# Gate, up and down products of a two-FFN layer as seven block products for eight

## The chip, the cores and the metric

The kernel runs on one core of a Trainium2 chip. The metric is device time in microseconds (us) of one launch. A core has a matrix engine (TensorE, PE), three engines for elementwise work (VectorE or DVE, ScalarE or ACT, GpSimd or POOL) and a queue engine (SyncE, SP) that issues the DMAs between DRAM and the on-chip memory SBUF. Matmuls write to eight PSUM banks of 128 x 512 fp32 words. Each engine runs its own instruction stream in order; semaphores order the engines against each other.

## What is computed

One layer over x of 1024 tokens x 1024 features, all fp32:

```
x = x + 1/2 * swiglu(rmsnorm(x, ffn1_norm), ffn1 weights)
x = x + attention(rmsnorm(x, mix_norm))       # 16 query heads, 4 key heads, window of 2 chunks of 64, sinks
x = x + 1/2 * swiglu(rmsnorm(x, ffn2_norm), ffn2 weights)
out = rmsnorm(x, final_norm)
swiglu(h) = (silu(h @ w_gate) * (h @ w_up)) @ w_down      # w_gate, w_up 1024 x 2816, w_down 2816 x 1024
```

## The kernel before

Every product is made with three passes of the engine's reduced fp32 type (fp32r): an operand is split into a high half (ACT copies it into fp32r) and a low half (DVE subtracts the high half from it), and high x high, high x low and low x high are added up in PSUM (`three_passes`, L391 is the matmul). The tokens are 8 tiles of 128, and two halves of 512.

An FFN is a loop over 11 groups of 256 hidden columns (`swiglu` on each engine). SP loads the 1024 x 256 blocks of the gate and up weights into `stage_g` and `stage_u` and 256 rows of the down weights into `stage_d`; ACT and DVE split them into `w` (`hi_of` L647, `lo_of` L951). PE makes four units per group (two column blocks f, two token halves), each of 48 matmuls: gate into one bank, up into another (`gate_up_unit`). For each unit `hidden` follows: ACT takes silu of the gate bank (L691), DVE multiplies it with the up bank (L1011), ACT and DVE split the result into `a_T` (L694, L1015). Then PE makes the group's share of the down product, 16 units of 6 matmuls (`down_unit`, 8 token tiles, 2 column halves), through a ring of four banks, and DVE adds each to x, which stays in SBUF (`add_to_x`, L1022). The first unit of the next group is put behind the down product.

Norms (index m, 8 tiles each for FFN1, attention, FFN2 and the end) are spread over four engines: POOL multiplies the tile of x with the norm's weights (`weigh`, L341), ACT sums the squares (L663) and takes the root (L668), DVE corrects it (`rstd`, L972 to L978), ACT or DVE scales (L675, L984), PE transposes by the identity (`turn`, L418), ACT and DVE split into `hT` (L683, L1003). The tiles of the first norm are interleaved with the first group's products; those of the attention's norm follow as the last group's tiles come out of the down product; those of FFN2's norm are turned while the attention's output product runs (`o_unit`), the last three inside `first_gate_up`. Attention itself (q, k, v products, scores, exp, probabilities times v, output product) is written out by hand as an interleaving of 16 steps, and its order is not touched by the change.

## Time and profile before

| | us |
|---|---|
| median of 3 runs | 1812.92 (1812.62 to 1813.11) |
| profiled execution, span from first to last instruction | 1812.2 |
| PE busy in it | 1760.0 (97%) |
| DVE busy | 809.5 (45%) |
| ACT busy | 493.7 (27%) |
| POOL busy | 133.0 (7%) |
| bytes moved by the DMA queues | 101.85 MB |

The profile is of one execution. Its own time is the span; what lies around it is the 0.7 us by which the median stands above. The engines work side by side, so the busy times don't add up to the span; what matters is which engine the others wait for. Start times in the rows are counted from the span's start. A few per cent of the matmul records can be missing, so a count in a timeline row may be a little short.

### The profile page before, as it was taken

How to read it: one execution, taken by the hardware profiler on the slowest of the kernel's cores; microseconds unless marked ns; L12 is line 12 of the kernel's file. 1: busy time of each engine (PE TensorE's matmuls, PEld its weight loads, DVE VectorE, ACT ScalarE, POOL GpSimd, SP SyncE). 2: the span in 40 equal slices, each digit the busy share in tenths (PEclk: the TensorE clock that was granted, in tenths of full speed). 3: DMA queues.
4: the chain of work that ended last, by engine and by line, in shares of the span. 5: the costliest groups of instructions: out<-in, count | busy, mean ns of one | idle time of the engine just before them, and what ended most of it. 6: DMA issues, size and time to landing. Idle time of an engine off the chain costs nothing.

```text
span 1812.2 us, 20835 instructions
## 1 busy us (share of the span) xinstructions
PE 1760.0 (97%) x8200; PEld 1464.0 (81%) x8200; DVE 809.5 (45%) x1226; ACT 493.7 (27%) x918; POOL 133.0 (7%) x82
## 2 busy tenths in 40 slices
PE   5999999999999999889999999999999999999996
PEld 4888888888888888778888878888888888888885
DVE  7433323424423332743689984343234244233326
ACT  4211111122111111532666653111111221111114
POOL 4000000000000000440221320000000000000003
PEclk9999999999999999999999999999999999999999
DMA  5212102102102201133212232121021021022002
GB/s 177 81 59 69 46 23 69 46 23 69 53 17 69 81 23 24 36 80 84 59 47 59 59 93 74 66 69 46 23 69 46 23 69 47 22 69 81 0 1 93
DMA packets 103751, 101.85 MB, mean 56 GB/s; under 512 B 37792, under 2 KB 93216, under 8 KB 103712
## 3 DMA queue, kind: packets, MB, share of 16 engines
q1 hardware_dynamic: 103712, 101.34, 18.3%
q8 instruction: 24, 0.39, 0.1%
q14 instruction: 15, 0.12, 0.0%
HBM read 97.13 MB, written 4.19 MB: 56 GB/s over the span
## 4 chain that ended last, share of the span: by engine, by line
PE 86%; DVE 11%; ACT 1%; issue 1%; DMA 0%; DVEq 0%; ACTq 0%
PE bank L391 84%; DVE x_res L1022 2%; DVE w L951 2%; DVE stat L978 2%; DVE hT L1003 1%; DVE stat L972 1%; PE bank L418 1%; PE bank L563 1%; DVE hT L1171 1%; DVE soft L1133 1%; DVE probs_T_lo L1158 1%; DVE hn L984 0%; PE bank L576 0%; ACT hT L683 0%; ACT junk L663 0%
## 5 line engine op out<-in xcount | busy, mean ns | idle before, releaser
L391 PE MATMUL bank<-hT,w 128*128 128x512 f32 (+1 forms) x4728 | 1078.8, 389 | 3.0 <-DVE hT L1003 1.6
L391 PEld LDWEIGHTS bank<-hT,w 128*128 128x128 f32 x4728 | 883.7, 188 | 186.2 <-issue 3.1
L391 PE MATMUL bank<-w,a_T 128*128 128x512 f32 x2112 | 484.7, 390 | 3.2 <-DVE x_res L1022 3.2
L391 PEld LDWEIGHTS bank<-w,a_T 128*128 128x128 f32 x2112 | 395.8, 188 | 86.9 <-DVE x_res L1022 4.9
L1011 DVE TENSOR_TENSOR a_full<-silu_g,bank 128x512 f32<-128x512 f32 x88 | 60.5, 688 | 682.8 <-ACT silu_g L691 682.6
L1022 DVE SCALAR_TENSOR_TENSOR x_res<-bank,x_res 128x512 f32<-128x512 f32 x416 | 278.0, 688 | 140.8 <-PE bank L391 140.5
L691 ACT ACTIVATE silu_g<-bank 128x512 f32<-128x512 f32 x88 | 52.7, 599 | 696.2 <-PE bank L391 696.2
L341 POOL TENSOR_TENSOR hn<-x_res,norm_w 128x1024 f32<-128x1024 f32 x31 | 77.8, 2521 | 1474.2 <-DVE x_res L1022 1454.3
L647 ACT ACTIVATE w<-stage_d 128x1024 fp32r<-128x1024 f32 x60 | 61.1, 1062 | 357.5 <-PE bank L391 357.5
L391 PE MATMUL bank<-w,hT 128*128 128x512 f32 (+1 forms) x576 | 120.3, 364 | 1.5 <-DVE x_res L1022 1.0
L391 PEld LDWEIGHTS bank<-w,hT 128*128 128x128 f32 x576 | 95.6, 194 | 17.4 <-DVE w L951 2.1
L1015 DVE TENSOR_TENSOR a_T<-a_full,a_T 128x512 fp32r<-128x512 f32 x88 | 61.0, 693 | 61.4 <-ACT a_T L694 61.4
L951 DVE TENSOR_TENSOR w<-stage_d,w 128x1024 fp32r<-128x1024 f32 x60 | 79.2, 1353 | 8.9 <-ACT w L647 8.7
L694 ACT ACTIVATE a_T<-a_full 128x512 fp32r<-128x512 f32 x88 | 55.6, 632 | 66.4 <-DVE a_full L1011 66.4
L418 PE MATMUL bank<-ident,hn 128*128 128x128 f32 x192 | 29.3, 302 | 31.6 <-DVE hn L984 19.1
L951 DVE TENSOR_TENSOR w<-stage_g,w 128x1024 fp32r<-128x1024 f32 x44 | 54.4, 1235 | 5.5 <-ACT w L647 5.2
L418 PEld LDWEIGHTS bank<-ident,hn 128*128 128x128 f32 x192 | 24.3, 155 | 37.5 <-issue 17.7
L951 DVE TENSOR_TENSOR w<-stage_u,w 128x1024 fp32r<-128x1024 f32 x44 | 53.6, 1219 | 0.0
L800 ACT ACTIVATE probs<-bank,soft 128x128 f32<-128x128 f32 (+1 forms) x128 | 45.0, 372 | 25.4 <-DVE soft L1137 25.4
L647 ACT ACTIVATE w<-stage_g 128x1024 fp32r<-128x1024 f32 x44 | 46.0, 1046 | 0.0
L647 ACT ACTIVATE w<-stage_u 128x1024 fp32r<-128x1024 f32 x44 | 45.9, 1044 | 0.0
L364 POOL TENSOR_TENSOR probs<-probs,soft_inv 128x512 f32<-128x512 f32 x32 | 33.9, 1068 | 109.9 <-DVE soft_inv L1146 109.6
(62 smaller groups left out, 675.7 us busy)
## 6 DMA issues: line engine op xcount, KB each, us to landing
stage_d<-in_ffn_w_down SPq DMA_DIRECT2D x22, 1024.0 KB, 4.9
stage_g<-in_ffn_w_gate SPq DMA_DIRECT2D x21, 1024.0 KB, 5.4
stage_u<-in_ffn_w_up SPq DMA_DIRECT2D x21, 1024.0 KB, 7.9
stage_d<-in_attn_w_o SPq DMA_DIRECT2D x32, 256.0 KB, 3.9
stage_qkv<-in_attn_w_qkv SPq DMA_DIRECT2D x32, 256.0 KB, 3.7
x_res<-in_x SPq DMA_DIRECT2D x8, 512.0 KB, 6.7
stage_qkv<-in_attn_w_qkv SPq DMA_DIRECT2D x8, 512.0 KB, 3.7
out_dram<-hn SPq DMA_DIRECT2D x7, 512.0 KB, 2.6
```

The costliest lines, as they stand in the source:

```text
L341: pool.tensor_tensor(hn[:, m % 4, :], x_res[:, t, :], norm_w[:, :], ALU.mult).then_inc(weighted, 1)
L391: mm = pe.matmul(psum, lhs, rhs, start=(first and n == 0 and v == 0), stop=(last and n == len(parts) - 1 and v == 2))
L418: mm = pe.transpose(banks[turn_bank(m) + k // 4][:, (k % 4) * P:(k % 4 + 1) * P], hn[:, m % 4, k * P:(k + 1) * P], ident[:, :])
L647: act.activation(slot_view, stage, ACT.Copy).then_inc(hi_done, 1)
L691: act.activation(silu_g[:, half, :], banks[2 * half][:, :], ACT.Silu).then_inc(silu_done, 1)
L694: act.activation(a_T[:, 0, f, half * HALF:(half + 1) * HALF], a_full[:, half, :], ACT.Copy).then_inc(a_hi_done, 1)
L800: act.activation(probs[:, b % 4, n, lo:], banks[s][:, n * P + lo:(n + 1) * P], ACT.Exp, bias=soft[:, NEG_MAX, b % 4, n:n + 1], accum_out=s ...
L951: dve.tensor_tensor(lo, stage, hi.bitcast(F32), ALU.subtract).then_inc(split_done, 1)
L978: dve.tensor_tensor(stat[:, RSTD, c], stat[:, R0, c], stat[:, CORR, c], ALU.mult).then_inc(rstd_done, tiles)
L1011: dve.tensor_tensor(a_full[:, half, :], silu_g[:, half, :], banks[2 * half + 1][:, :], ALU.mult).then_inc(gate_up_free, 1)
L1015: dve.tensor_tensor(a_T[:, 1, f, cols], a_full[:, half, :], a_T[:, 0, f, cols].bitcast(F32), ALU.subtract).then_inc(a_ready, 1)
L1022: dve.scalar_tensor_tensor(out=cols, in0=banks[4 + bank_][:, :], scalar=factor, in1=cols, op0=ALU.mult, op1=ALU.add).then_inc(ring_free, 1)
```

## The change

The three large products of each FFN are made by Strassen's scheme in Winograd's form. The left operand is cut into 2 x 2 blocks (A11, A12, A22 and the sums S1 to S4; A21 enters only in sums), the right one likewise, and seven products of forms (product k takes form k, in the order A11, A12, S2, S3, S1, A22, S4) give all four result blocks, summed in two PSUM banks with copies between.

- *Gate and up.* The normed activations, 1024 tokens x 1024, are cut at 512 tokens and 512 features. Their seven forms (`forms`, 128 x 7 x 2 x 4 x 512) are built once per FFN: POOL makes S3, S2, S1, S4 in natural order (`natural_sums`), PE transposes each 128 x 512 piece (`turn_unit`, 28 per FFN), ACT and DVE split it. The tiles are normed in place in x_res (the first four) and in hn, so x is loaded again later, in FFN2 from a copy that is written to DRAM (`x_mid`, `spill_x`). The weight forms of each group are built by DVE from the stages (`slot_sums`) and split (`slot_hi_of`, `slot_lo_of`). A group is 14 steps (7 products k, 2 matrices m) of 12 matmuls. ACT copies a running sum from its bank (`copy_part`), DVE adds the other bank to it (`sum_block`), then silu and product give the four hidden blocks (`silu_block`, `hidden`).
- *Seven forms of the hidden activations.* DVE makes the sums (`hidden_sums`, `hidden_last_sum`), and SP stores all seven forms of each group to DRAM (`hidden_forms`), 256 KB each.
- *Down.* It is no longer part of the groups but a phase behind all 11 of them: 7 products of 11 steps, each step 12 matmuls over four banks (`down`, `down_tile`). SP loads the hidden block of each step back through a ring of six; the whole down matrix is loaded in four quarters (`load_down_w`), and POOL makes their sums (`down_sums`, 44 of 128 x 512 per FFN). The last six steps run tile by tile. x gets 28 additions per FFN (`add_down`) for 176.
- The tiles 0 to 3 and 4 to 7 finish at different products, and the norm behind each FFN follows that order.

The core of the diff:

```diff
+PRODUCTS = 7
+HI_BEFORE = [0, 2, 6, 4, 8, 10, 12]
+LO_BEFORE = [0, 2, 8, 4, 6, 10, 12]
+STEPS = PRODUCTS * GROUPS
+SPLITS = 6
+LAST_STEPS = STEPS - SPLITS
+DOWN_TO = [(0, 0), (0, 0), (1, 0), (1, 1), (1, 1), (1, 0), (0, 1)]
...
@@ sync
-            def load_groups(gate, up, down, s0):
-
-                with sp.Fori(0, GROUPS - 1) as i:
-                    sp.wait_ge(split_done, i * 6 + (s0 + 4))
-                    load_gate_up(gate, up, i * GROUP + GROUP)
-                    sp.wait_ge(split_done, i * 6 + (s0 + 6))
-                    load_down(down, i * GROUP + GROUP)
+            def group(q, i, g0):
+                sp.wait_ge(slot_ready, nth(i, 14, 14 * (GROUPS * q + g0 + 1)))
+                load_stage(q, i * GROUP + (g0 + 1) * GROUP)
+                for part in range(3):
+                    stores(q, i, g0, part)
...
+                for n in range(SPLITS, STEPS):
+                    down_consumed(sp, q, n - SPLITS)
+                    if n == SPLITS or n % GROUPS == 0:
+                        sp.wait_ge(buf_stored[BUF_OF[n // GROUPS]], 16 * GROUPS * (q + 1))
+                    load_a(q, n)
+                    if n in (6, 10, 14):
+                        load_down_w(q, B12, (n - 6) // 4)
+                    if n in (8, 12, 16):
+                        load_down_w(q, B22, (n - 8) // 4)
+                    if n in (7, 9, 11, 13, 24, 26, 28, 30):
+                        half, j = divmod([7, 9, 11, 13, 24, 26, 28, 30].index(n), 4)
+                        t = j + 4 * (half if q else 1 - half)
+                        if q:
+                            sp.wait_ge(spilled[t], 16)
+                        load_x(source, t)
...
@@ gpsimd
+            def natural_sums(q, j):
+                n = 16 * q + 4 * j
+                h1, h2 = h_of(q, N_FFN[q] + j), h_of(q, N_FFN[q] + 4 + j)
+                pool.wait_ge(hn_done, N_FFN[q] + 4 + j + 1)
+                if j:
+                    pool.wait_ge(form_turned, UNITS * q + 8 + 5 * j)
+                pool.tensor_tensor(nat[:, NAT_OF[S3], :], h1[:, 0:HALF], h2[:, 0:HALF], ALU.subtract
+                                   ).then_inc(nat_done, 1)
...
+            def first_forms(q):
+                for j in range(6):
+                    weigh_form(q, j)
+                natural_sums(q, 0)
+                weigh_form(q, 6)
+                natural_sums(q, 1)
+                weigh_form(q, 7)
+                natural_sums(q, 2)
+                natural_sums(q, 3)
...
+            def down_sums(q):
+                done = 4 * GROUPS * q
+                ready = 2 * STEPS * q
+                for g in range(GROUPS):
+                    pool.wait_ge(down_w_loaded[B12][g // 4], 16 * (q + 1))
+                    pool.wait_ge(down_w_loaded[B22][g // 4], 16 * (q + 1))
+                    pool.tensor_tensor(down_w[B12][:, g, :], down_w[B22][:, g, :], down_w[B12][:, g, :], ALU.subtract
+                                       ).then_inc(down_w_summed, 1)
+                    pool.wait_ge(down_w_summed, done + 2 * g + 1)
+                    pool.wait_ge(down_ready, ready + 2 * (g + 1))
+                    pool.tensor_tensor(down_w[B11][:, g, :], down_w[B12][:, g, :], down_w[B11][:, g, :], ALU.add
+                                       ).then_inc(down_w_summed, 1)
...
@@ tensor
+                if k == 0 and first and q:
+                    pe.wait_ge(exp_done, 32)
+                elif k == 0 and not first:
+                    pe.wait_ge(hidden_done if m else silu_done, nth(i, 4, 4 * n))
+                elif k == 1 and not first:
+                    pe.wait_ge(block_summed, nth(i, 6, 6 * n - 1 + m))
+                elif k in (2, 4, 6):
+                    pe.wait_ge(part_copied, nth(i, 6, 6 * n + k - 1 + m))
+                elif k in (3, 5):
+                    pe.wait_ge(block_summed, nth(i, 6, 6 * n + k - 2 + m))
+                three_passes(banks[y_bank if k in (1, 3, 5) else x_bank][:, :],
+                             [((slot[q][k][m][:, 0, kt, :], slot[q][k][m][:, 1, kt, :]),
+                               (forms[:, k, 0, kt, :], forms[:, k, 1, kt, :])) for kt in range(4)],
+                             k in (0, 1, 3), k in (1, 5, 6)).then_inc(gate_up_done, 1)
...
+            def down(q, between):
+                for n in range(LAST_STEPS):
...
+                    pe.wait_ge(down_ready, 2 * STEPS * q + 2 * (n + 1))
+                    for j in range(4):
+                        down_tile(q, n, j)
+                for j in range(4):
+                    if between is not None:
+                        between(j)
+                    for n in range(LAST_STEPS, STEPS):
+                        if j == 0:
+                            pe.wait_ge(down_ready, 2 * STEPS * q + 2 * (n + 1))
+                        down_tile(q, n, j)
...
@@ vector
+            def group(q, i, g0, first=False, last=False):
+                if not first:
+                    sum_block(q, i, g0, 0, 0)
+                    sum_block(q, i, g0, 0, 1)
+                hidden(q, i, g0, 0)
+                if not last:
+                    slot_lo_of(q, i, g0 + 1, 0)
+                    slot_lo_of(q, i, g0 + 1, 1)
+                    slot_sums(q, i, g0 + 1, 3)
+                    slot_sums(q, i, g0 + 1, 2)
+                sum_block(q, i, g0, 1, 0)
+                sum_block(q, i, g0, 1, 1)
+                hidden(q, i, g0, 1)
...
+            for n in range(TT):
+                if n < 5:
+                    down_lo_of(1, 72 + n)
+                if n >= 4:
+                    add_down(1, 6, n - 4)
+                variance(N_FINAL + n)
+                rstd(N_FINAL + n)
```

## Rows read from the trace of the kernel before

**Rows 1.** Page, parts 1 and 2: busy us, share, instructions; PE in 40 slices.

```profile
PE 1760.0 (97%) x8200; PEld 1464.0 (81%) x8200; DVE 809.5 (45%) x1226; ACT 493.7 (27%) x918; POOL 133.0 (7%) x82
...
PE   5999999999999999889999999999999999999996
```

**Rows 2.** Page, part 4: the chain of waits by engine and by line.

```profile
PE 86%; DVE 11%; ACT 1%; issue 1%; DMA 0%; DVEq 0%; ACTq 0%
PE bank L391 84%; DVE x_res L1022 2%; DVE w L951 2%; DVE stat L978 2%; DVE hT L1003 1%; DVE stat L972 1%; PE bank L418 1%; PE bank L563 1%; DVE hT L1171 1%; DVE soft L1133 1%; DVE probs_T_lo L1158 1%; DVE hn L984 0%; PE bank L576 0%; ACT hT L683 0%; ACT junk L663 0%
```

**Rows 3.** Timeline of PE, 100 to 235 us: start, length, instructions, idle before.

```profile
144.00 21.92 PE L391 MATMUL bank<-w,a_T 128*128 128x512 f32 x96
165.76 43.68 PE L391 MATMUL bank<-hT,w 128*128 128x512 f32 x192
209.28 21.92 PE L391 MATMUL bank<-w,a_T 128*128 128x512 f32 x96
```

**Rows 4.** Groups by line and shape: busy us, mean ns, idle before and its releaser.

```profile
L1015 DVE TENSOR_TENSOR a_T<-a_full,a_T 128x512 fp32r<-128x512 f32 x88 | 61.0, 693 | 61.4 <-ACT a_T L694 61.4
L694 ACT ACTIVATE a_T<-a_full 128x512 fp32r<-128x512 f32 x88 | 55.6, 632 | 66.4 <-DVE a_full L1011 66.4
...
L951 DVE TENSOR_TENSOR w<-stage_g,w 128x1024 fp32r<-128x1024 f32 x44 | 54.4, 1235 | 5.5 <-ACT w L647 5.2
...
L364 POOL TENSOR_TENSOR probs<-probs,soft_inv 128x512 f32<-128x512 f32 x32 | 33.9, 1068 | 109.9 <-DVE soft_inv L1146 109.6
```

**Rows 5.** Timeline of ACT and of DVE in one group.

```profile
176.84 0.60 ACT L691 ACTIVATE silu_g<-bank 128x512 f32<-128x512 f32 x1 [7.57 <-PE bank L391]
...
177.47 0.69 DVE L1011 TENSOR_TENSOR a_full<-silu_g,bank 128x512 f32<-128x512 f32 x1 [8.06 <-ACT silu_g L691]
```

**Rows 6.** DMA issues (KB, us to landing); window 0 to 20 (last: DMA share, GB/s).

```profile
stage_g<-in_ffn_w_gate SPq DMA_DIRECT2D x21, 1024.0 KB, 5.4
stage_u<-in_ffn_w_up SPq DMA_DIRECT2D x21, 1024.0 KB, 7.9
...
0.00:20.00 20.00, 2.59 (x11) 2.22 (x12) 13.50 (x17) 6.73 (x14) 12.70 (x11) 1.00 0.97 305
```

**Rows 7.** Timeline of the start, POOL and PE.

```profile
6.74 12.00 POOL L341 TENSOR_TENSOR hn<-x_res,norm_w 128x1024 f32<-128x1024 f32 x5 [5.27 <-DMA norm_w<-in_ffn_norm]
...
45.92 24.35 PE L391 MATMUL bank<-hT,w 128*128 128x512 f32 x106 [0.91 <-DVE hT L1003]
```

**Rows 8.** Timeline of PE between FFN1 and the q and k products.

```profile
777.70 1.97 PE L418 MATMUL bank<-ident,hn 128*128 128x128 f32 x8 [5.40 <-DVE hT L1003]
...
779.32 5.09 PE L391 MATMUL bank<-w,hT 128*128 128x256 f32 x24
...
784.25 1.04 PE L418 MATMUL bank<-ident,hn 128*128 128x128 f32 x8
...
785.05 3.12 PE L391 MATMUL bank<-w,hT 128*128 128x256 f32 x24
...
788.00 12.20 PE L391 MATMUL bank<-hT,w 128*128 128x512 f32 x53
```

**Rows 9.** Timeline where the attention's output product ends and FFN2 starts.

```profile
1065.00 1.06 ACT L663 ACTIVATE junk<-x_res 128x1024 f32<-128x1024 f32 x1 [1.55 <-DVE x_res L1022]
...
1072.37 1.64 PE L391 MATMUL bank<-w,hT 128*128 128x512 f32 x6
...
1086.11 14.09 PE L391 MATMUL bank<-hT,w 128*128 128x512 f32 x61
```

**Rows 10.** Timeline of the end: the last addition to x.

```profile
1804.17 0.67 DVE L1022 SCALAR_TENSOR_TENSOR x_res<-bank,x_res 128x512 f32<-128x512 f32 x1
```

**Rows 11.** Timeline of DVE and POOL where both work.

```profile
735.54 4.55 DVE L951 TENSOR_TENSOR w<-stage_qkv,w 128x1024 fp32r<-128x1024 f32 x2
...
735.71 3.30 POOL L341 TENSOR_TENSOR hn<-x_res,norm_w 128x1024 f32<-128x1024 f32 x1 [702.36 <-DVE x_res L1022]
...
1778.56 4.77 POOL L341 TENSOR_TENSOR hn<-x_res,norm_w 128x1024 f32<-128x1024 f32 x2 [700.50 <-DVE x_res L1022]
...
1780.01 0.69 DVE L1022 SCALAR_TENSOR_TENSOR x_res<-bank,x_res 128x512 f32<-128x512 f32 x1
```

More of the change, by code:

```diff
@@ new lines, in trunk @@
+    probs_T_lo = at("probs_T_lo", 204, [P, 2, 4 * P], F32R)
+    norm_w = at("norm_w", 208, [P, D])
+    q_T = {key: at(f"q_T{key[0]}{key[1]}", 96 + 8 * slot, [P, HALF // CHUNK, 4, CHUNK])
+           for key, slot in Q_SLOT.items()}
+    forms = at("forms", 32, [P, PRODUCTS, 2, 4, HALF], F32R)
+    stage = [at("stage_g", 144, [P, KD, GROUP]), at("stage_u", 152, [P, KD, GROUP])]
+    early = [[168, 172], [176, 180], [160, 164]]
+    low, high = [[0, 4], [8, 12]], [[16, 20], [24, 28]]
+    slot_kb = [early + low + high, early + high + low]
@@ L206, in trunk, with nth, h_of, down_consumed @@
         wo_view = w_o.rearrange("(i s e p) n -> i s e p n", i=2, s=2, e=4)
+        def nth(i, per, start):
+            return i * per + start
+        def h_of(q, m):
+            j = m - N_FFN[q]
+            return x_res[:, tile_of(m), :] if j < 4 else hn[:, j - 4, :]
+        def down_consumed(engine, q, n):
+            p, g = divmod(n, GROUPS)
+            if g == GROUPS - 1:
+                engine.wait_ge(down_full, 28 * q + 4 * p + 4)
+            else:
+                engine.wait_ge(down_step, (LAST_STEPS - 6) * q + (GROUPS - 1) * p + g + 1)
         block = ctx.enter_context(nc.Block())
@@ new lines, in feed_forward @@
+            def feed_forward(q):
+                first_pairs(q)
+                group(q, 0, 0, first=True)
+                with act.Fori(0, GROUPS - 2) as i:
+                    group(q, i, 1)
+                group(q, 0, GROUPS - 1, last=True)
+            act.wait_ge(started, 1)
+            act.activation(stat[:, R0, 0:1], stat[:, RSTD, 0:1], ACT.Sqrt)
+            for j in range(4):
+                act.wait_ge(x_loaded[tile_of(j)], 16)
+                square_to(j, junk[:, :])
+                if j >= 1:
+                    root(j - 1)
+                if j >= 2:
+                    scale_in(j - 2, h_of(0, j - 2))
@@ L744, in _ @@
+            root(3)
+            form_hi_of(0, 0)
+            form_hi_of(0, 1)
+            scale_in(2, h_of(0, 2))
+            form_hi_of(0, 2)
+            form_hi_of(0, 3)
+            scale_in(3, h_of(0, 3))
+            for v in range(4, 8):
+                form_hi_of(0, v)
+            slot_hi_of(0, 0, 0, 0, True)
+            slot_hi_of(0, 0, 0, 1, True)
+            feed_forward(0)
             loads = [0, 0]
@@ new lines, in _ @@
+            scale_mix(1)
+            down_hi_of(0, 74)
+            root(N_MIX + 2)
+            square_mix(3)
+            scale_mix(2)
+            down_hi_of(0, 75)
+            root(N_MIX + 3)
+            scale_mix(3)
+            down_hi_of(0, 76)
+            hi_qkv(0)
+            hi_qkv(1)
+            norm_back(0)
+            norm_back(1)
+            for t in range(4, TT):
+                square_mix(t)
+                root(N_MIX + t)
+                if t < 6:
+                    norm_back(t - 2)
+                scale_mix(t)
+                if t >= 6:
+                    norm_back(t - 2)
@@ L774, in shift_v @@
+            hi_qkv(2)
+            norm_back(6)
+            norm_back(7)
             def shift_v(half):
@@ new lines, in feed_forward @@
+            def feed_forward(q):
+                group(q, 0, 0, first=True)
+                with dve.Fori(0, GROUPS - 2) as i:
+                    group(q, i, 1)
+                group(q, 0, GROUPS - 1, last=True)
+                for n in range(SPLITS, 72):
+                    if n % GROUPS == SPLITS and n > SPLITS:
+                        for j in range(4):
+                            add_down(q, n // GROUPS - 1, j)
+                    down_lo_of(q, n)
+                for j in range(4):
+                    add_down(q, 5, j)
```

1225 lines of the change are left out of this document (727 added, 498 removed).

## The prediction

> **What bounds the kernel now.** I read the page's busy times first [rows 1]: TensorE (PE) is busy for 97% of the span, and the 40 slices show full stretches broken only at the start, between 720 and 780 us, and at the end. VectorE (DVE) is at 45%, ScalarE (ACT) at 27%. The chain of waits agrees [rows 2]: 86% of it is PE, 84% the three-pass matmuls of L391. So the kernel is bound by the number of 128x512 matmuls, and everything else counts only where PE waits. The PE timeline gives the price [rows 3]: from 165.76 to 209.28 us run 192 gate and up matmuls, from 144.00 to 165.76 run 96 down matmuls, both at 226.67 ns each with no gap. A group of 256 hidden columns is 288 of them, 65.28 us; one FFN is 11 groups, 718.1 us.
>
> **What the seven products remove.** A group has 7 products x 2 matrices x 4 contraction tiles x 3 passes = 168 matmuls of the same shape for 192. The down product, now a phase after all groups, has 7 x 11 steps x 4 tiles x 3 passes = 924 for 1056. One FFN falls from 3168 to 2772, or 396 x 0.22667 = 89.8 us; two give **-179.5**. An FFN's floor is 628.3 us.
>
> **The group loop, cost 0.** A group is 14 steps of 12 matmuls, 2.72 us each, 38.08 in all. DVE gets 36 instructions of 128x512 (14 low halves, 8 weight sums, 6 block sums, 4 products, 4 hidden sums); at 0.69 [rows 4] that is 24.8 us. ACT gets 24, 15.1 us at 0.63 [rows 4], with one table load. Neither fills 38.08, and POOL is idle, so the order of the waits decides. The tightest is product 5 after product 4: the running sum must be copied from its bank (ACT) and added to the other bank (DVE) before PE may write that bank, while PE has one step, 2.72 us, in between. The trace has such a handoff: a unit that PE left at 176.64 is read by ACT from 176.84, and DVE starts at 177.47, 0.03 after ACT ended [rows 5]. So 0.20 + 0.63 + 0.69 = 1.5 us, slack 1.2. I followed both queues in program order over one group, with the sums of the next group's weights between; each arrives 1.2 us or more before PE needs it. The weights of the next group are asked for 5.6 us into a group, land at 11 and 13.5 by the landing times [rows 6], and are wanted at 17. Bounds: 0, and 1 us a group (22 us) where that slack is used up; I take 0, as the handoffs of the loop of before never reach PE [rows 3].
>
> **The first group of each FFN, +7.** There the previous group's tail does not exist: the last slot is ready only about 17 us into the group, the 2 MB land 8 us later, and ACT's copies and DVE's sums stand behind them in their queues. Product 5 then starts at 30.8 us of group time for 27.2, 3.6 us late, twice. Bounds 0 and 12.
>
> **The start of FFN1, +20.** Before, PE went on with the second unit at 45.92, having done 48 matmuls (10.9 us): effective start 35.0 [rows 7]. After, product 2 needs all four S2 forms, and these come from POOL: 8 norm products of 128x1024, 2.40 each (five in 12.00) [rows 7], and 16 half-width sums. The trace has no such sum: half of 2.40 is 1.20, the 128x512 product with soft_inv took 1.07 [rows 4]; I take 1.20. ACT carries squares, scales, eight form copies and four slot copies before the second four tiles; with the DVE steps between held up by POOL that is an estimate of 28 us. Two more norm products end at 34.3, the first scaled tile of the second half stands at 35.6, then POOL has 16 x 1.20 + 2 x 2.40 = 24.0 to do: 59.6, and product 2 starts 2 us later (slot split). Four steps of PE are done by then: effective start 50.7, +15.7. Against it: DVE has twelve instructions with both inputs in SBUF in this stretch, 8.3 us, that exclude POOL (next part); I take 3. And PE has idled: after 5.40 us of idle the next 24 matmuls of 128x256 took 5.09 where 24 later took 3.12 [rows 8], 1.2 for 2.4 GHz; I take 1.3. Sum +20. Lower bound 13 (1.07 each, no interference), upper 27.
>
> **The start of FFN2, +17.** Before, the remaining units start at 1086.11, effective start 1075.2, and the attention's output product ended at 1074.0: the next norm was hidden but for 1.2 us [rows 9]. After, tile 4 is squared from 1065.00 as now [rows 9], two norm products and a held-up DVE step put the first scaled tile at 1073.2, and the same 24.0 us of POOL end at 1097.2. With 2 for the slot, 3 for interference and 1 for the clock, less 10.9 for four steps under it: 1092.3, +17. Bounds 10 and 24. This is cover that the old order had and the new one gives up.
>
> **Into attention, -15.** Before, FFN1's work would have ended at 35.0 + 718.1 = 753.1, and the q and k products start at 788.00 [rows 8], 34.9 us later, for 4 v units (785.05 to 788.00: 2.95) and 8 transposed tiles (784.25 to 785.05: 0.80), 18.2 us. The rest is PE waiting for norms of tiles that end 2.72 us apart. After, tiles 0 to 3 are complete one product (30 us) earlier, and the last four end 4.1 us or more apart, about the 4 us that a norm takes, with v units between. I take 15 of the 16.7; bounds 10 and 17. **The end, -10.** Before, from 1075.2 + 718.1 = 1793.3 to 1812.2 is 18.9. After, four tiles are normed early and the last add starts 0.3 after PE; from the last add's start to the end were 8.0 us [rows 10]. With 0.6 of queue 8.9. Bounds 7 and 10.6. The attention between is the same: 0.
>
> **The down phase, +10 an FFN, +20.** A step is 2.72 us; DVE has 2 instructions for it (1.4 us), ACT 2. Three things are late there.
> (a) Transfers, 4: between steps 6 and 16 SP issues 11 hidden blocks (2.9 MB), 6 chunks of down weights (5.8 MB) and 4 tiles of x (2.1 MB), 10.8 MB in 27 us, behind some 9 us of backlog. The fullest stretch of before moved 305 GB/s at a DMA share of 0.97 [rows 6]; 10.8 MB take 35 us. The six-deep ring covers all but about 4. Bounds 0 and 5.
> (b) POOL against DVE, 3. At 735.54 DVE's two low halves took 4.55 (2 x 1.24 on the mean [rows 4]) while POOL's product took 3.30 for 2.40: one waited for the other, then the other way round [rows 11]. An add from PSUM took its 0.69 under a running POOL product [rows 11]. So an instruction with both inputs in SBUF and a POOL sum exclude each other. All of this phase's low halves are such, and POOL has 44 sums: while POOL has work, two DVE instructions cost up to 2 x (1.20 + 0.69) = 3.8 us for a step of 2.72. The ring hides some, chunk arrivals space POOL. Bounds 0 and 9.
> (c) Product 6, 3: the last five steps' low halves stand between the norms of four finished tiles, whose POOL products hold DVE 2.4 each; all six last steps must be ready for the first tile. Followed in order, the last is ready up to 5.5 late. Bounds 0 and 5.5.
> Together 0 to 20 an FFN, I take the middle, 10. The Trainium skill (DMA: Bandwidth & Descriptors, Specifications) puts the limit of a core's memory at about 358 GB/s. By that (a) would be nothing and the sum 8 lower; the 305 of the row is the measured one, and stands.
>
> **Sum.** 1812.2 - 179.5 + 7 + 20 + 17 - 15 - 10 + 20 = 1671.7 against the profiled execution, whose span of 1812.2 is 0.7 under the median of 1812.92. Forecast **1672 us**, 7.8% less. All lower bounds together give 1629, all upper ones 1741.
>
> **Rivals.** *Everything covered* (0.12): POOL's chain at its lower bounds, a down phase without a stall: 1812.9 - 179.5 + 13 + 10 - 17 - 10 + 4 = 1633. For it: the slack of PE's neighbours. Against: the chains of the starts are counted instructions on one engine.
> *The down phase paced by DVE behind POOL* (0.15): 44 POOL sums each paired with one DVE instruction are 83 us, in which DVE serves 22 steps, 60 us of PE: 23 lost, with (a) and (c) 33 an FFN, so 1672 + 2 x 23 = 1718. For it: the row at 735.54. Against: POOL waits for chunks and for split steps, so its sums don't stand back to back. The Trainium skill (SBUF — State Buffer, Who interferes with whom) calls this an exclusive lock held for a whole instruction; the trace agrees, 4.55 us for 2.4.
> *The group loop held by queue order* (0.12): 2 us a group where one late copy delays product 5, 22 x 2 = 44, 1716. For it: 36 + 24 instructions in two strict orders. Against: the slack of 1.2 us.
> *Slower than before* (0.02): DVE bound in the group loop. Break-even is a group of 38.08 + 141/22 = 44.5 us, or 1.24 us for each of the 36 instructions in place of 0.69; at 1.32 it would be 47.5 and the kernel 1879. For it: they read stages in pieces of 128 columns, never in the trace at this width. Against: a low half over such pieces at twice the width took 1.24 [rows 4], and half the width should not take the same.
> *The matmuls do not fall as counted, or each takes longer* (0.01): 1812.
>
> **Chances.** My forecast, with 1650 to 1700 as its own range, has 0.58. The range for 8 in 10 is 1640 to 1720: it cuts most of the covered case and ends just beyond the two dear ones. Within 0.2% (3.6 us) is what a measurement can't tell from no change. Faster 0.97, same 0.01, slower 0.02.
>
> **What would show it.** Right: 2772 matmuls per FFN at 0.227; loop groups of 38.1 us; PE waiting at both starts for forms whose maker is POOL; the q and k products under 20 us after FFN1's last; in the down phase, PE waits on DVE low halves in steps 9 to 30 and 71. Wrong: a loop group above 39 us, starts later than 27 us beyond the old ones, or down phases over 230 us (floor 209.4).

## The result, and the profile after

| | before | after |
|---|---|---|
| median (lowest to highest) of four runs each, us | 1813.01 (1812.62 to 1814.69) | 1727.25 (1725.97 to 1728.17) |
| span of the profiled execution, us | 1812.2 | 1724.0 |

The ratio of the times is 0.9524, 95% interval 0.9511 to 0.9538: 4.8% faster, where 7.8% was forecast. The forecast's span of 1671.7 us was missed by 52.3, and 1727 lies beyond the range of 1640 to 1720.

The page of the kernel after: busy times, PE in 40 slices, the chain of waits by engine, and four groups (busy us, mean ns, idle before).

```profile
PE 1625.4 (94%) x7480; PEld 1336.9 (78%) x7480; DVE 1114.5 (65%) x1752; ACT 725.2 (42%) x1463; POOL 311.3 (18%) x202
...
PE   4799999999998999799999996999999999989996
...
PE 74%; DVE 18%; ACT 3%; DMA 3%; issue 2%; POOL 0%; DVEq 0%; SPq 0%; ACTq 0%
...
L573 PE MATMUL bank<-forms,slot 128*128 128x512 f32 x3696 | 849.6, 392 | 9.6 <-DVE slot L1347 5.8
...
L573 PE MATMUL bank<-b_ring,a_ring 128*128 128x512 f32 x1848 | 437.6, 396 | 24.6 <-DVE b_ring L1391 24.5
...
L1388 DVE TENSOR_TENSOR a_ring<-a_raw,a_ring 128x512 fp32r<-128x512 f32 x154 | 142.6, 926 | 125.0 <-ACT a_ring L938 125.0
...
L1391 DVE TENSOR_TENSOR b_ring<-down_w,b_ring 128x512 fp32r<-128x512 f32 x154 | 144.5, 938 | 0.0
```

3696 and 1848 matmuls are 2772 an FFN, as counted. PE's share fell from 97% to 94%, with shallow dips at both starts, in both down phases, behind FFN1 and at the end, and DVE's part of the chain rose from 11% to 18% [rows 1, 2]. The place to look stands in the last two groups: a low half of 128x512 takes 0.93 us on the mean, where the same shape took 0.69 before [rows 4]. The two groups hold 308 of them, and PE waited 24.5 us for them.

PE's timeline gives a ledger. "Effective start" is the time at which an FFN would have begun had its 11 groups run at 38.08 us each up to the first down matmul. Every line is in us of the profiled executions.

| stretch | predicted | measured | off |
|---|---|---|---|
| effective start of FFN1, first group included | 58.5 | 486.33 - 418.9 = 67.4 | +8.9 |
| down phase of FFN1, its four transposed tiles (3.2) included | 222.6 | 486.33 to 725.08: 238.8 | +16.1 |
| to the q and k products | 16.7 | 725.08 to 745.16: 20.1 | +3.4 |
| q and k to the end of the output product | 286.0 | 288.8 | +2.8 |
| from there to the effective start of FFN2 | 21.7 | 1033.97 to 1066.0: 32.0 | +10.3 |
| down phase of FFN2 | 219.4 | 1484.91 to 1715.7: 230.8 | +11.4 |
| the end | 8.9 | 8.3 | -0.6 |
| sum | | | +52.3 |

So 27.5 of the 52.3 are in the two down phases and 19.2 in the two starts. Inside FFN1's down phase the loss sits in two places. The first: PE between 525 and 561 us (start, length, count, idle before), then DVE and POOL in 5 us of it.

```profile
525.35 3.02 PE L573 MATMUL bank<-b_ring,a_ring 128*128 128x512 f32 x12 [0.37 <-DVE b_ring L1391]
...
540.30 3.02 PE L573 MATMUL bank<-b_ring,a_ring 128*128 128x512 f32 x12 [0.39 <-DVE b_ring L1391]
...
560.70 9.59 PE L573 MATMUL bank<-b_ring,a_ring 128*128 128x512 f32 x41 [0.34 <-DVE b_ring L1391]
```

```profile
536.38 1.61 POOL L519 TENSOR_TENSOR down_w<-down_w,down_w 128x512 f32<-128x512 f32 x1
536.77 1.77 DVE L1388 TENSOR_TENSOR a_ring<-a_raw,a_ring 128x512 fp32r<-128x512 f32 x1
...
537.96 1.75 POOL L515 TENSOR_TENSOR down_w<-down_w,down_w 128x512 f32<-128x512 f32 x1
...
538.47 1.78 DVE L1391 TENSOR_TENSOR b_ring<-down_w,b_ring 128x512 fp32r<-128x512 f32 x1
...
540.17 1.77 DVE L1388 TENSOR_TENSOR a_ring<-a_raw,a_ring 128x512 fp32r<-128x512 f32 x1
...
541.36 18.74 POOL L524 TENSOR_TENSOR down_w<-down_w,down_w 128x512 f32<-128x512 f32 x11
```

A step takes 3.40 us instead of 2.72. DVE's low halves start every 1.70 us, and between two of their starts lies exactly one start of a POOL sum: the two engines take turns, one instruction each. POOL's last back-to-back sum ends at 560.1 (541.36 and 18.74), and the row at 560.70 is the first with no further gap. The second place is product 6, the last six steps: PE there, then DVE ahead of the first wait and in a later step.

```profile
692.28 1.94 PE L701 MATMUL bank<-ident,hn 128*128 128x128 f32 x8 [3.45 <-ACT hn L872]
...
698.46 0.96 PE L573 MATMUL bank<-b_ring,a_ring 128*128 128x512 f32 x3 [0.40 <-DVE b_ring L1391]
702.88 1.65 PE L573 MATMUL bank<-b_ring,a_ring 128*128 128x512 f32 x3 [3.46 <-DVE b_ring L1391]
707.05 1.65 PE L573 MATMUL bank<-b_ring,a_ring 128*128 128x512 f32 x3 [2.52 <-DVE b_ring L1391]
```

```profile
683.49 2.88 DVE L1391 TENSOR_TENSOR b_ring<-down_w,b_ring 128x512 fp32r<-128x512 f32 x1
686.90 1.75 DVE L1281 SCALAR_TENSOR_TENSOR stat<-stat 128x1 f32<-128x1 f32 x1 [0.27 <-ACT stat L865]
...
688.88 2.08 DVE L1287 TENSOR_TENSOR stat<-stat 128x1 f32<-128x1 f32 x1
...
697.11 0.69 DVE L1388 TENSOR_TENSOR a_ring<-a_raw,a_ring 128x512 fp32r<-128x512 f32 x1 [2.00 <-ACT a_ring L938]
```

PE waits for the first normed tile, then for each step's low half. Up to 690.93 POOL's norm products (four in 10.33 us from 680.60) hold DVE up to 2.9 us an instruction, a product of one column among them. From then on the low halves have their 0.69 again, and it is the order of the queues that delays them: ACT makes a step's high halves only behind the square and the scaling of a tile, DVE waits 2.00 us for them (the row at 697.11), and the steps come 4.2 to 4.4 us apart. After the long waits three matmuls took 1.65 us, at a granted clock of 0.50 (1.2 GHz), where three took 0.96 after a short one, at 1.00 (2.4 GHz); the mean from 688.70 to 725.08 was 0.77.

### The profile page after: what moved, and what is told of

It reads as the page before. It is cut to its first block, busy times and chain, and to the rows that moved or that the text cites. A ratio compares the mean times of both kernels' runs of the same rounds, so it can differ in the third digit from the quotient of the medians.

```text
span 1724.0 us, 22342 instructions
## 1 busy us (share of the span) xinstructions
PE 1625.4 (94%) x7480; PEld 1336.9 (78%) x7480; DVE 1114.5 (65%) x1752; ACT 725.2 (42%) x1463; POOL 311.3 (18%) x202
## 4 chain that ended last, share of the span: by engine, by line
PE 74%; DVE 18%; ACT 3%; DMA 3%; issue 2%; POOL 0%; DVEq 0%; SPq 0%; ACTq 0%
PE bank L573 71%; DVE b_ring L1391 4%; DVE a_ring L1388 3%; DVE x_res L1627 1%; DVE slot L1347 1%; DMA a_raw<-hidden_forms 1%; DVE w L1268 1%; DVE forms L1305 1%; DMA stage_u<-in_ffn_w_up 1%; DVE stat L1281 1%; DVE stat L1287 1%; PE bank L773 1%; DVE x_res L1403 1%; DVE hT L1616 1%; DVE soft L1579 1%
## 5 line engine op out<-in xcount | busy, mean ns | idle before, releaser
L573 PE MATMUL bank<-forms,slot 128*128 128x512 f32 x3696 | 849.6, 392 | 9.6 <-DVE slot L1347 5.8
L573 PEld LDWEIGHTS bank<-forms,slot 128*128 128x128 f32 x3696 | 699.9, 190 | 157.5 <-DVE slot L1347 7.0
L573 PE MATMUL bank<-b_ring,a_ring 128*128 128x512 f32 x1848 | 437.6, 396 | 24.6 <-DVE b_ring L1391 24.5
L573 PEld LDWEIGHTS bank<-b_ring,a_ring 128*128 128x128 f32 x1848 | 349.2, 191 | 110.9 <-DVE b_ring L1391 39.1
L1388 DVE TENSOR_TENSOR a_ring<-a_raw,a_ring 128x512 fp32r<-128x512 f32 x154 | 142.6, 926 | 125.0 <-ACT a_ring L938 125.0
L1391 DVE TENSOR_TENSOR b_ring<-down_w,b_ring 128x512 fp32r<-128x512 f32 x154 | 144.5, 938 | 0.0
L1347 DVE TENSOR_TENSOR slot<-raw,slot 128x512 fp32r<-128x512 f32 x176 | 116.5, 713 | 1.6 <-ACT slot L902 1.6
L573 PE MATMUL bank<-hT,w 128*128 128x512 f32 x480 | 113.7, 393 | 0.0
L573 PEld LDWEIGHTS bank<-hT,w 128*128 128x128 f32 x480 | 88.8, 188 | 19.2 <-DVE w L1268 0.3
L902 ACT ACTIVATE slot<-raw 128x512 fp32r<-128x512 f32 x176 | 98.2, 622 | 0.1
```

Source lines behind the costliest of these rows:

```text
L573: mm = pe.matmul(psum, lhs, rhs, start=(first and n == 0 and v == 0), stop=(last and n == len(parts) - 1 and v == 2), skip_group_check=True)
L902: act.activation(slot[q][k][m][:, 0, :, :], src, ACT.Copy).then_inc(slot_hi, 1)
L1347: dve.tensor_tensor(slot[q][k][m][:, 1, :, :], src, slot[q][k][m][:, 0, :, :].bitcast(F32), ALU.subtract).then_inc(slot_ready, 1)
L1388: dve.tensor_tensor(a_ring[r][:, 1, :], a_raw[r][:, :], a_ring[r][:, 0, :].bitcast(F32), ALU.subtract).then_inc(down_ready, 1)
L1391: dve.tensor_tensor(b_ring[r][:, 1, :], src, b_ring[r][:, 0, :].bitcast(F32), ALU.subtract).then_inc(down_ready, 1)
```

## The experiments

Each kernel is the one after with the edit shown. Its lines may be moved by a few. A time without a range is of one execution; four executions of one of these kernels lie 1.4 to 3.4 us apart, so differences of 2 us are read from the rows and not from the times.

**e1: fills with zero in place of the down sums**, so this kernel leaves the 44 sums of an FFN out.

```diff
-                    pool.tensor_tensor(down_w[B12][:, g, :], down_w[B22][:, g, :], down_w[B12][:, g, :], ALU.subtract
-                                       ).then_inc(down_w_summed, 1)
+                    pool.memset(down_w[B12][:, g, :], 0.0).then_inc(down_w_summed, 1)
...
```

> The 44 sums of down weights per FFN on POOL are replaced by fills of the same tiles with zero (same waits, same counts, nothing read), so the down product is not the reference's. Theory A (exclusion): a POOL instruction that reads SBUF and a DVE instruction with both inputs in SBUF shut each other out. Then DVE's low halves of the ring fall from 1.78 to 0.69 us in steps 7 to 24, PE's steps 14 to 24 from 3.40 to 2.72, and each down phase is 9 us shorter: 1727 - 18 = 1709 (1706 to 1712). Rival B (transfers): the ring ran empty because of the loads between steps 6 and 16; the fills change nothing there: 1727. Rival C (results): PE waits for the sums' results; the fills are shorter but come at the same chunk landings: 1722 to 1727.

Measured: 1707.76 us, span 1705.7: theory A. **e2: the same sums on DVE**, each ahead of or behind the low halves of the step that frees its block, POOL without them; this kernel computes the whole layer.

```diff
                 for n in range(SPLITS, 72):
+                    p, g = divmod(n, GROUPS)
+                    if p == 1:
...
+                        w_sum(B12, g, B22, B12, ALU.subtract, 0)
+                    if p == 2:
+                        w_sum(B21, g, B21, B11, ALU.subtract, 2 * g + 2, GROUPS + g + 1)
...
                     down_lo_of(q, n)
+                    if p == 1:
+                        w_sum(B11, g, B12, B11, ALU.add, 2 * g + 1, g + 1)
+                    if p == 3:
+                        w_sum(B12, g, B22, B11, ALU.subtract, 2 * g + 2, n + 1)
```

> The same 44 sums moved from POOL to DVE, between its low halves, one or two per step (complete kernel). Theory A (exclusion): DVE has 2 low halves and at most 2 sums per step, 4 x 0.69 = 2.8 us in product 1 where the ring was 5 steps ahead, 2.1 after; nothing excludes it any more. Down phases 7 to 9 us shorter each: 1709 to 1713. Rival B (transfers set it): 1727 or more, since DVE now also waits for the chunks. If DVE's own queue becomes the limit in product 1 (11 x 0.1 us and the waits): 1714 to 1720.

Measured: 1708.75 us, span 1707.0, theory A again, and once more:

> The same kernel as e2_dve_sums (the 44 sums of an FFN's down weights on DVE in place of POOL), timed in three rounds: 1708 to 1710 us, ratio to the kernel before 0.942, interval wholly below that of the change itself (0.9511 to 0.9538).

Measured: 1708.41 us (1707.2 to 1708.6, four runs), ratio to before 0.9418 (0.9402 to 0.9433), against 0.9511 to 0.9538 for the change. First PE in e1, and DVE where POOL's memsets run; then PE and DVE in e2 (its second run), in the same stretch; then two windows of e2 (busy of PE, PEld, DVE, ACT, POOL; granted clock, DMA share, GB/s).

```profile
485.85 84.48 PE L569 MATMUL bank<-b_ring,a_ring 128*128 128x512 f32 x372
...
532.43 0.53 POOL L522 MEMSET down_w<- 128x512 f32 x1 [2.03 <-DVE b_ring L1387]
...
532.78 0.69 DVE L1384 TENSOR_TENSOR a_ring<-a_raw,a_ring 128x512 fp32r<-128x512 f32 x1 [0.47 <-ACT a_ring L934]
```

```profile
486.01 84.26 PE L571 MATMUL bank<-b_ring,a_ring 128*128 128x512 f32 x371
...
533.72 0.68 DVE L1389 TENSOR_TENSOR b_ring<-down_w,b_ring 128x512 fp32r<-128x512 f32 x1
534.32 1.28 DVE L1491 TENSOR_TENSOR down_w<-down_w,down_w 128x512 f32<-128x512 f32 x2
```

```profile
486.00:525.35 39.35, 39.35 (x175) 32.59 (x174) 25.43 (x43) 14.55 (x27) 0.00 (x0) 1.00 0.98 356
525.35:560.70 35.35, 35.35 (x158) 29.27 (x157) 33.80 (x57) 14.87 (x27) 0.00 (x0) 1.00 0.49 157
```

In both, PE runs without a gap from the first down matmul; the rows end with the window asked for, and in FFN1 the first wait comes only after 71 of the 77 steps, 193 us on. That holds though DVE is busy 96% of the second window in e2. The same 44 additions cost 9.2 us an FFN on an engine that seemed free and nothing in PE's rows on the one that seemed loaded: on DVE a sum takes 0.64 (two in 1.28), on POOL it took 1.7 and made one low half 1.77 long for 0.69. The transfers were the same in e1 and e2, so they were not the cause.

**e3: high and low halves of the last steps ahead of the norms**, on ACT and DVE, and PE's transposes behind each tile instead of ahead of it.

```diff
                 for j in range(4):
-                    if between is not None:
-                        between(j)
                     for n in range(LAST_STEPS, STEPS):
...
+                    if between is not None:
+                        between(j)
...
+            for n in range(72, STEPS):
+                down_lo_of(0, n)
             for t in range(4):
-                down_lo_of(0, 72 + t)
                 variance(N_MIX + t)
```

> In product 6 the high and low halves of steps 72 to 76 are put before the norms of the four finished tiles, on ACT and DVE; on PE the transposes of these norms come after each tile's steps instead of before (FFN1). Theory N (norm queue): the last six steps lose 16.9 us in FFN1 and 12.1 in FFN2 (6.9 of waits, the rest at the lower clock after them); both fall to 0 to 4: 1727 - 24 = 1703 (1699 to 1709). Rival (the norms only move the wait): PE then waits at the transposes in FFN1 for as long, and gains only in FFN2: 1715.

Measured: 1725.23 us, span 1723.2, above theory N's 1703 and its rival's 1715. The theory fell as a sum, though its step came true: PE ended product 6 at 715.1 instead of 725.2. It then stood idle. PE in e3 behind FFN1, and DVE's additions to x at the end of FFN2:

```profile
710.74 4.35 PE L573 MATMUL bank<-b_ring,a_ring 128*128 128x512 f32 x18
...
723.54 5.49 PE L573 MATMUL bank<-w,hT 128*128 128x256 f32 x24 [7.58 <-DVE x_res L1396]
...
745.81 14.57 PE L573 MATMUL bank<-hT,w 128*128 128x512 f32 x63
```

```profile
1704.48 0.69 DVE L1396 SCALAR_TENSOR_TENSOR x_res<-bank,x_res 128x512 f32<-128x512 f32 x1
1708.05 0.69 DVE L1396 SCALAR_TENSOR_TENSOR x_res<-bank,x_res 128x512 f32<-128x512 f32 x1
...
1715.19 0.69 DVE L1396 SCALAR_TENSOR_TENSOR x_res<-bank,x_res 128x512 f32<-128x512 f32 x1
```

The additions come at the pace of the norms ahead of them in DVE's queue, 3.57 us a tile, from 1704.48 on (1696.61 in the next kernel, where they stand earlier). PE ended 4.9 us sooner, at 1711.0, and from there to the end it took 12.2 us for 8.2. The q and k products start at 745.81, no sooner than the 745.16 of the kernel after, and attention took 2 us longer, in the wait for an addition to x ahead of the last of the output product (5.35 us for 4.03) and at the lower clock behind it (12 matmuls in 5.43 us for 4.58); why that wait was longer stays open. **e7: e3, and these additions one norm step earlier.**

```diff
+                if t in (1, 3):
+                    add_down(0, 6, t // 2)
...
             for n in range(TT):
-                if n >= 4:
-                    add_down(1, 6, n - 4)
                 variance(N_FINAL + n)
+                if n in (3, 4, 6):
+                    add_down(1, 6, {3: 1, 4: 2, 6: 3}[n])
                 rstd(N_FINAL + n)
+                if n == 1:
+                    add_down(1, 6, 0)
```

> The kernel e3_lo_first (high and low halves of the last five steps ahead of the norms) with one more edit: the adds that take product 6 out of its banks stand one norm step earlier on DVE, so they no longer wait behind the scaling factor of another tile. In e3 the PE's waits inside product 6 had gone, and after the last tile PE stood idle 7.58 us at 723.54 behind the last add at 722.79, and at the end the first add came only at 1704.48, six us after its tile, with the others 3.57 us apart. Theory D (the gain of e3, about 10 us in FFN1 and 5 in FFN2, was given back at the handover by the order of DVE's queue): the v units start at about 717.5 in place of 723.5 and the final chain ends about 8.3 us after PE's end (1710.8), 4 us sooner: span 1723.2 - 4 for the tail, and up to - 5 for attention: 1714 to 1719. Rival N (the handover is paced by the norm chain of the tiles itself, about 4.6 us a tile on ACT and DVE, whatever the adds do): only the tail's 4 us or less, and q and k products start where they did, span 1719 to 1723.

Measured: 1719.93 us, span 1717.9. That is in theory D's range, but not by its steps. DVE's first and last addition at the end, then PE behind FFN1:

```profile
1696.61 0.69 DVE L1396 SCALAR_TENSOR_TENSOR x_res<-bank,x_res 128x512 f32<-128x512 f32 x1
...
1709.89 0.69 DVE L1396 SCALAR_TENSOR_TENSOR x_res<-bank,x_res 128x512 f32<-128x512 f32 x1
```

```profile
712.08 1.10 PE L701 MATMUL bank<-ident,hn 128*128 128x128 f32 x8 [1.89 <-DVE hT L1515]
...
723.53 5.46 PE L573 MATMUL bank<-w,hT 128*128 128x256 f32 x24 [5.36 <-issue]
...
744.46 15.91 PE L573 MATMUL bank<-hT,w 128*128 128x512 f32 x69
```

PE now ends at 1707.5, 10.4 us before the end: the tail is 1.8 us shorter than in e3, where 4 were forecast, and still 2.2 longer than in the kernel after. The other 3.6 of the 5.3 us under e3 lie ahead of FFN2's down phase: the q and k products start 1.4 sooner, and attention takes 288.6 us, as in the kernel after. Behind FFN1 the additions are no longer what it waits for: the last `hT` of tile 3, in DVE from 722.16 for 1.27, ends 0.1 before the v unit starts. DVE's product for the scaling factor of tile 5 stands ahead of it, 2.08 long under a norm product of POOL. By these rows the norms pace this stretch, as rival N says. **e8: e7, with POOL's norm products after all low halves.**

```diff
+            pool.wait_ge(down_ready, 2 * STEPS)
             for t in range(TT):
                 pool.wait_ge(down_free, 20 + t + 1)
...
+            pool.wait_ge(down_ready, 4 * STEPS)
             for n in range(TT - 1):
```

> e7_early_adds with POOL made to wait with the norm products of the finished tiles (L473) until all low halves of the down phase are made, in both FFNs. In e3 these products (8.44 us for three at 682.97) held three low halves at 2.9 us each where 0.68 is one alone, and PE waited 1.67 us there. Theory X (POOL's norm products exclude DVE's low halves and this is what is left of the waits in product 6): low halves of steps 72 to 76 take 0.7 us each, PE waits under 0.5 us between step 72 and the end of product 6, and about 1.5 us an FFN are gained over e7 where the norm chain still comes in time. Rival: the norm chain starts later and the transposes and v units wait for it: no gain over e7, or up to 3 us worse. Time against the kernel before: ratio about 0.945 to 0.950 in the first case.

Measured: 1727.50 us (1726.48 to 1729.56, four runs), ratio 0.9527 (0.9511 to 0.9543), span 1725.2, 7.3 above e7 and no different from the change. PE in e8 in product 6 of FFN1, then a low half of it:

```profile
692.89 0.96 PE L575 MATMUL bank<-b_ring,a_ring 128*128 128x512 f32 x3 [1.39 <-DVE b_ring L1386]
698.92 1.94 PE L703 MATMUL bank<-ident,hn 128*128 128x128 f32 x8 [5.06 <-ACT hn L874]
```

```profile
692.15 0.68 DVE L1386 TENSOR_TENSOR b_ring<-down_w,b_ring 128x512 fp32r<-128x512 f32 x1
```

Theory X is right on the mechanism (all ten low halves of FFN1's last five steps take 0.68 or 0.69) and wrong on the gain: the norm products now stand on the path, as its rival said. PE waits 5.06 us for the first normed tile, and at the end of FFN2, where PE ends at 1707.4 as in e7, the tail is 17.8 us for 10.4.

**The starts. e4: POOL's sums of the activation forms on an eighth of the columns**, the rest of the forms left out.

```diff
-                pool.tensor_tensor(nat[:, NAT_OF[S3], :], h1[:, 0:HALF], h2[:, 0:HALF], ALU.subtract
+                pool.tensor_tensor(nat[:, NAT_OF[S3], 0:E8], h1[:, 0:E8], h2[:, 0:E8], ALU.subtract
...
```

> POOL's 16 sums of normed activations per FFN are made on 64 of 512 columns (the rest of the forms is stale, so the result is not the reference's), same waits and order. Theory P (POOL's chain sets both starts): each sum falls from 1.27 to about 0.3, product 2 starts 14 us or more earlier (57 instead of 71.5 in FFN1): 1727 - 28 = 1699 (1694 to 1703). Rival Q (the loop through DVE: a transpose waits for the form copied four units before it, whose low half stands behind six weight sums on DVE, and POOL waits for the transpose): 32 DVE instructions, 21 us, stay, product 2 starts at 62 to 66: 1708 to 1716.

Measured: 1722.19 us, span 1720.4. Product 2 of FFN1 begins at 67.76 for 71.48: the sums shrank from 1.27 to 0.33 us each, 15 us of work gone an FFN, and 3.7 came of it there. That is far from theory P's 14, and short of rival Q's 62 to 66 and 1708 to 1716 too; what Q says of the transposes is seen below. **e6: the first group's slot sums behind the third pair's low halves.**

```diff
                     rstd(m + 2 + j)
+                pair(2)
                 for k in (3, 2, 4):
                     slot_sums(q, 0, 0, k, True)
-                pair(2)
```

> The kernel after with one reordering on DVE in each FFN's first forms: the six sums of the first group's slots (L1337, 52.94 to 58.70 in the trace after) go behind the five low halves of the third pair of tiles instead of ahead of them. Theory L (the starts are set by a loop: a low half stuck behind these sums keeps a bank from PE's transposes, the transposes keep POOL's next natural sums back, gap 4.27 us at 60.69 for FFN1 and 4.88 at 1062.24 for FFN2): the gap goes and product 2 starts 3 to 4 us earlier in each FFN (71.48 becomes about 68, 1073.02 about 1069.5), span 1724.0 - 7 = 1717, time 1720. Rival S (the sums are themselves on the way to product 2, through the slot copies and low halves): what the transposes gain, the slots lose, product 2 starts within 1 us of 71.48, time 1727. Against both: the span is longer, over 1729, if the slot of product 3 comes after product 2 has ended.

Measured: 1727.15 us, span 1725.1, as rival S says. In the kernel after (first fence) the loop is there: DVE's six slot sums (from 52.94 to 58.77, two of them held by POOL's sums) hold a low half, that holds PE, that holds POOL. In e6 (second) POOL's gap is 0.92 us for 4.27 and its chain ends 3.7 us sooner, and the transposes then wait longer, behind the same sums and the slots' low halves.

```profile
53.55 1.75 DVE L1337 TENSOR_TENSOR raw<-stage_u 128x512 f32<-128x512 f32 x1
...
59.43 1.12 PE L607 MATMUL bank<-ident,nat 128*128 128x128 f32 x4 [3.91 <-DVE forms L1305]
...
60.69 1.27 POOL L489 TENSOR_TENSOR nat<-x_res,hn 128x512 f32<-128x512 f32 x1 [4.27 <-PE bank L607]
...
71.48 2.93 PE L573 MATMUL bank<-forms,slot 128*128 128x512 f32 x6 [1.89 <-DVE slot L1347]
```

```profile
61.24 1.72 POOL L496 TENSOR_TENSOR nat<-x_res,nat 128x512 f32<-128x512 f32 x1
...
67.77 1.12 PE L607 MATMUL bank<-ident,nat 128*128 128x128 f32 x4 [5.26 <-DVE forms L1305]
...
70.77 3.78 PE L573 MATMUL bank<-forms,slot 128*128 128x512 f32 x8 [1.88 <-DVE slot L1347]
```

**e10: those slot sums as memsets, so the first group's sums are left out; e11: e10 and e4 together.**

```diff
-                    dve.tensor_tensor(raw[q][k][m][:, :, :], src, src2, op).then_inc(slot_sum, 1)
+                    if first:
+                        dve.memset(raw[q][k][m][:, :, :], 0.0).then_inc(slot_sum, 1)
...
```

> The kernel after, with the eight sums of the first group's slots of each FFN (L1337, DVE, both inputs in SBUF) replaced by memsets of the same outputs on the same engine behind the same waits, so the combinations of gate and up weights of that one group are left out. Theory V (the starts are set by DVE's work, which stood busy 11.15 of the 12 us from 60 to 72 us and 22.78 of the 24 from 1050 to 1074): the eight sums held DVE about 8 us an FFN, a part of it by exclusion with POOL's natural sums; product 2 starts 4 to 6 us earlier in each FFN (71.48 becomes 66 to 67, 1073.02 becomes 1067 to 1069), span 1712 to 1717. Rival O (POOL's chain and the transposes set the start, DVE only fills their gaps): product 2 within 1.5 us of 71.48, span 1721 to 1724.

Measured: 1724.08 us, span 1722.0, product 2 at 68.42. The result lies between the two: 3.1 us for the 4 to 6 of theory V, and a span in the rival's range.

> e10_slots_memset and e4_eighth together: the first groups' slot sums as memsets and POOL's 16 natural sums an FFN on 64 of their 512 columns (the rest of those forms is left out). By theory V the two gains mostly add, since each takes time off DVE (the sums themselves, and what POOL's sums hold of it): e4 alone began product 2 at 67.76, so about 62 to 63 here, span 1708 to 1713. If instead both only shorten one chain that ACT's copies limit (four form copies, six slot copies and four more in order), product 2 starts no earlier than 65 and the span is 1714 or more.

Measured: 1720.54 us, span 1718.8, product 2 at 66.67, the second case. ACT and PE in e11:

```profile
59.16 3.23 ACT L904 ACTIVATE slot<-raw 128x512 fp32r<-128x512 f32 x6
...
62.27 2.06 ACT L883 ACTIVATE forms<-bank 128x512 fp32r<-128x512 f32 x4
...
63.85 1.12 PE L609 MATMUL bank<-ident,nat 128*128 128x128 f32 x4 [3.00 <-DVE forms L1307]
...
66.67 19.21 PE L575 MATMUL bank<-forms,slot 128*128 128x512 f32 x72 [1.71 <-DVE slot L1352]
```

With POOL's sums near nothing and the slot sums as memsets, 4.8 us are gained in FFN1, and 5.2 in the whole span. What then stands on the path is read from these rows, not shown by a run: ACT's last form copies wait behind six slot copies in its queue, and a low half and a bank behind them.

**e12: the down sums on DVE (e2) and the order of product 6 (e7) in one kernel**; its diff is theirs.

> A complete kernel of the edits that paid: the 44 down weight sums an FFN on DVE (e2_dve_sums, 1708.4 us) with the order of product 6 of e7_early_adds (1719.9 us, 7.3 under the change). The two act in different stretches (steps 11 to 44, and from step 66 on), so the gains should add: 1708.4 - 7 = 1701 us, ratio to the kernel before 0.938, between 0.936 and 0.940. If DVE's extra sums were late in the last steps too, less: 1705.

Measured: 1700.72 us (1699.29 to 1702.69, four runs), ratio to before 0.9383 (0.9367 to 0.9398), span 1697.4. The gains add (18.8 and 7.3 us in the medians, 26.5 together), and this kernel, which computes the whole layer, is faster than both: its interval lies below that of e2 and of the change. The last row of PE and the last addition in it:

```profile
1670.67 16.98 PE L571 MATMUL bank<-b_ring,a_ring 128*128 128x512 f32 x66 [1.81 <-DVE b_ring L1382]
...
1689.17 0.69 DVE L1394 SCALAR_TENSOR_TENSOR x_res<-bank,x_res 128x512 f32<-128x512 f32 x1
```

## Why the prediction was wrong

The sign, the counts and the group loop were right, and they carry the gain: 2772 matmuls an FFN at 0.227 us. From product 5 of the first group (92.94) to the first down matmul (486.33) are 393.4 us, where 11 groups less the first ten steps of the first (418.9 - 27.2) make 391.7. The rival of queue order in the group loop (44 us) is out.

**The step that failed is the down phase, "Together 0 to 20 an FFN, I take the middle, 10".** It came to 26.1 in FFN1 (238.75 less 209.4 and 3.2) and 21.4 in FFN2, beyond its upper bound. Both phases are over the 230 us that I had named as a sign of being wrong. Two of its three terms were too small, (c) by most, and (a) was there for nothing:

- *(b) POOL against DVE*, 3 forecast, 9.2 an FFN by e1 (18.3 in the spans, both together). PE's rows say the same: 8.2 and 8.8 from the first wait on DVE on, and 0.9 and 0.4 ahead of it. The rival "the down phase paced by DVE behind POOL" is what happened in kind, at 3.4 us for two low halves and two sums where it had 3.8, but not in size: it had 23 us an FFN. (Its 33 an FFN is a slip as well: 23 with 4 and 3 is 30, which gives 1712 and not 1718.) I set it aside because "POOL waits for chunks and for split steps, so its sums don't stand back to back". That held for the last 11 of the 44 sums only. The chunks and the low halves that the others wait for were always there in time: from its first at 504.66 on, 33 sums stood back to back to 560.1. The Trainium skill (SBUF — State Buffer, Who interferes with whom) calls the two engines' shared access a lock held for a whole instruction. The rows at 536.38 to 540.17 show the engines taking turns, one for one, at 1.70 us a pair; I had cited it and then priced it away.
- *(a) Transfers*, 4 forecast, nothing measured: in e1 and e2, with the same transfers, PE has no gap up to the last six steps. I had divided by 305 GB/s [rows 6]. In this phase the queues moved 356 GB/s at a share of 0.98 (the first window of e2 above; 359 in the kernel after). The limit of about 358 from the Trainium skill (DMA: Bandwidth & Descriptors, Specifications), by which this term "would be nothing", agrees with that number. A share of 0.97 in the rows of before was thus no proof of the highest rate.
- *(c) Product 6*, 3 forecast, 16.9 in FFN1 and 12.1 in FFN2. I had followed the low halves and left out three things that the rows show: each step's high halves wait in ACT's queue for a tile's square and scaling, so that a step comes only every 4.2 to 4.4 us; PE itself waits for the first normed tile (3.45); and after each long wait it runs at the lower clock, which makes about 7 of the 16.9, the waits being 9.8. That POOL's norm products hold DVE was in the sum; it lasted to 690.93 only. e3, e7 and e8 show that most of it is no free loss: whatever PE gains there, the norms behind take back in FFN1. From the start of FFN2's down phase to the end, e7 takes 5.3 us less.

**The starts**, +20 and +17 forecast, with the first group +3.5 each, came out 8.9 and 10.3 longer: 28.9 and 27.3 without the first group's part, above their bounds of 27 and 24 and over the 27 that I had named as a sign of being wrong. By my steps product 2 of FFN1 would start at 59.6 + 3 + 2 = 64.6, and it started at 71.48. The duration of a sum was right (1.27 for 1.20), the chain was not. I counted POOL alone. It stood still 4.27 and 4.88 us for PE, which stood for DVE, and in FFN2 its first sum began 2.9 us after the output product where I had its input 0.8 before. In FFN1 e4 removes 15 us of POOL's work and gains 3.7; e6 removes most of the gap and gains 0.7; e11 gains 4.8. So neither POOL's sums nor DVE's slot sums set it alone; by the rows the chain runs through four engines, but no run shortened the part of ACT or PE, and what sets the rest stays open. The clock added to it: 72 matmuls from 71.48 took 19.23 us, not 16.3, and 1.3 of these 2.9 were in the sum.

**Into attention** was 3.4 us longer than predicted, with the 15 us gain thus 11.6: by the rows a norm takes 4.6 us for the 4 that I took (in e3, where the tiles wait for nothing else, the additions between them start at 710.06, 714.74 and 719.36). The stretch from the q and k products to the end of the output product, "the same", took 2.8 more. In it is a wait of 4.03 us for an addition to x (L1627) at 1001.92, where the kernel before waited 0.79 and 0.22: four norm products of POOL for FFN2 (9.41 us from 991.15) hold a step of DVE ahead of it, 2.27 us at 998.32. **The end** was right within 0.6.

## What to carry to other kernels

Before work is given to an idle engine, ask whether its instructions and those of the loaded one both have all operands in SBUF, as POOL's sums and DVE's low halves have here. Then work on the idle engine can cost the other more than doing it itself: each sum on POOL made a low half 1.1 us longer, and on DVE the sum takes 0.64. When a phase waits on a chain that was only reordered, look at the next phase before pricing the gain: moved waits come back at the next handover. And where an operation has a chain over several engines, follow each engine's queue through it; the sum of one engine's instructions is only a lower bound.

## What the runs showed of the hardware

- Under strict alternation a 128x512 fp32 low half takes 1.75 to 1.78 us in the record for 0.69 alone, and POOL's sum 1.6 to 1.75 for 1.27: a pair every 1.70 us. Undisturbed, low halves start 0.60 apart (from 560.57) and POOL's sums 1.23 (from 36.91), 1.83 together, so a pair costs slightly less than both in turn.
- A memset was out of the exclusion on either side: in e1 the low half at 532.78 began under a memset of POOL and took its 0.69, and in e10 six DVE memsets took 3.19 from 53.22 on beside two sums of POOL, which kept their 1.27.
- An addition from PSUM kept its own length beside POOL: four of them 2.47 at 532.02 in the kernel after.
- A one-column product of DVE, 0.16 alone, took 2.08 under a norm product of POOL (the row at 688.88): the price was set by what holds, not by the size of what is held.
